# Low parts of eleven weight units per layer formed by accumulating transfers, and memsets that wait for the entry normalisation

## The chip, the cores and the metric

One core of a Trainium2 chip runs the whole program. The core has five engines with their own in-order instruction streams: PE (TensorE, the matmuls), DVE (VectorE), ACT (ScalarE), POOL (GpSimd) and SP, which here only issues transfers. The metric is the device time of one execution in microseconds (us); lower is better. Engines meet only through semaphores: an instruction waits until a counter has reached a value.

## The reference

Four normalisations and two layers over 512 tokens (two sequences of 256) of width 1024, all in float32. Each layer, cut to what matters here:

```
proj = h @ w_in                      # q, k, v, z, x/B/C, dt
attn = window_attention(rope(q), rope(k), v, sink)
xbc  = silu(depthwise_conv5(xbc))    # 12 tiles of 128 channels
y    = ssd(forward) + ssd(backward) + D * xs      # state space, chunks of 128
ssd_out = rms_norm(y * silu(z)) 
h = layer_norm(alpha * h + concat(attn, ssd_out) @ w_out)
h = layer_norm(alpha * h + (silu(conv3(h @ w_gate)) * (h @ w_val)) @ w_down)
```

## The kernel before

**Weights in units.** All weight matrices are cut into units of 128 x 1024 floats (512 KB). A layer has 105 units, numbered from 0: dt, k, v and q (0 to 6), the twelve convolved tiles (7 to 18), z (19 to 26), the output projection (27 to 38), up (39 to 82) and down (83 to 104). A ring of five slots (`RING = 5`) holds units in three forms: `raw` as loaded, `whi` (its rounded high part) and `wlo` (what is left, `raw - whi`). Each product is three matmuls: high by high, high by low, low by high. SP loads unit m into its slot once PE has finished unit m - 5 (`unit_used`); ACT copies `raw` into `whi` (function `split`, L595); DVE subtracts to give `wlo` (function `split`, L1285); PE waits for the count `unit_split` and multiplies.

**Slots.** A list of steps, `SCHED`, is written by `mixer_schedule`; each engine walks the same list and takes the steps that concern it, in that order. One slot n of the list surrounds the matmuls of unit n (step "G"). "SH" is ACT's high copy of a later unit (n + 4), "SL" DVE's low part, "S" both. In slots 19 to 26 of a layer (the z units) the state space part runs beside the projection. For each of its eight pairs i (a group of heads and a token block):

- SB (PE, L1166) and SF (PE, L1177) write exponents into four PSUM banks,
- SC (DVE, L1559, two instructions) caps them into `e_fwd` and `e_bwd`; SE (ACT, L759 twice and L765) takes the exponentials `e_fwd`, `e_bwd`, `e_off`,
- SW (DVE, L1564 and L1568) adds the two and multiplies by `cb`; SO (DVE, L1574) multiplies `e_off`,
- SD (PE, L1193) uses the results; SY (DVE, L1583) adds them up; SG (DVE, L1593) gates with z.

SB of pair i + 1 waits for all three exponentials of pair i. SD waits for SW and SO of its pair. A convolved tile goes: PE's product, ACT's centre tap (L693), four tap instructions on DVE (L1448), tanh on ACT ("SILU", L728), a product on DVE ("SIL2", L1455), and then a transposition on PE ("T", L1132), whose result ACT copies out (L746). POOL multiplies the same tile by D ("XS", L564) and builds the tiles `heads` ("MV", L575), 128 x 1024 each, in slots 15 to 17.

**Entry.** DVE normalises four token blocks of `hb` (L1342, L1345; `ln_normed` counts them), PE transposes them (L1033, L972), and POOL forms low parts (L531) and then clears three tiles with memsets (L546 to L548).

## Time and profile before

| what | value |
|---|---|
| median of 3 runs | 1307.52 us (1306.7 to 1307.57) |
| the profiled execution | 1307.72 us, of which the span is 1305.9 |
| PE busy | 1291.5 us (99% of the span) |
| DVE, ACT, POOL busy | 823.5, 580.6, 96.6 us |
| transfers | 129.24 MB, mean 99 GB/s |
| TensorE's granted clock | full speed, mean 0.999 |

The span is the time between the first and the last instruction; the 1.8 us beside it are around the program. The busy time of PE has modelled ends, so a stall shows as idle time only where it is longer than the tail of the matmul before it; the waits that the profile names are read for that.

### The profile page before, as it was taken

To read this page: it belongs to the slowest core of one execution; us is meant where nothing else is said; L and a number is where in the kernel's file an instruction comes from. 1 tells how busy PE (TensorE), PEld (TensorE's weight loads), DVE (VectorE), ACT (ScalarE), POOL (GpSimd) and SP (SyncE) were. 2 spreads that over 40 slices of the span, in tenths; PEclk is the share of its full clock that TensorE was granted. 3 is DMA by queue.
4 is the path that set the end of the run, shared out by engine and by line. 5 is a ranking of instruction groups with operands and counts; after the bars stand their busy time and mean duration, and the time that the engine had idled before them with its cause. 6 is when DMAs were issued, how large, how long until landed. Compare 5 with 4: busy or idle time off the path is not lost.

```text
span 1305.9 us, 16383 instructions
## 1 busy us (share of the span) xinstructions
PE 1291.5 (99%) x6688; PEld 1066.9 (82%) x6688; DVE 823.5 (63%) x1109; ACT 580.6 (44%) x875; POOL 96.6 (7%) x87
## 2 busy tenths in 40 slices
PE   9999999999999999999999999999999999999997
PEld 8877777889888888888898777778888888888886
DVE  7888799966444444342378987999654444443425
ACT  5766655436333333311276665544453333332112
POOL 2013400001000000000020234000000000000000
PEclk9999999999999999999999999999999999999999
DMA  5422212523333333333133212143233333333332
GB/s 188 163 68 56 65 59 65 182 62 126 96 97 98 96 99 95 128 98 97 55 129 135 65 50 81 52 143 113 82 98 97 98 97 97 97 97 128 98 97 112
DMA packets 33787, 129.24 MB, mean 99 GB/s; under 512 B 3793, under 2 KB 4209, under 8 KB 32561
## 3 DMA queue, kind: packets, MB, share of 16 engines
q1 hardware_dynamic: 33552, 127.91, 30.8%
q8 instruction: 53, 0.87, 0.3%
q0 software_dynamic: 160, 0.29, 0.1%
q14 instruction: 22, 0.17, 0.0%
HBM read 121.89 MB, written 6.29 MB: 98 GB/s over the span
## 4 chain that ended last, share of the span: by engine, by line
PE 90%; DVE 7%; issue 1%; ACT 1%; DMA 0%; DVEq 0%
PE ps L843 17%; PE ps L845 16%; PE ps L844 16%; PE ps L980 9%; PE ps L982 9%; PE ps L981 9%; PE ps L869 4%; PE ps L1193 1%; PE ps L1207 1%; PE ps L1217 1%; PE ps L1227 1%; DVE e_fwd L1559 1%; PE ps L972 1%; DVE e_fwd L1564 1%; DVE e_off L1574 1%
## 5 line engine op out<-in xcount | busy, mean ns | idle before, releaser
L843 PE MATMUL ps<-hhi,whi 128*128 128x512 f32 x1040 | 409.5, 394 | 0.0
L845 PE MATMUL ps<-hhi,wlo 128*128 128x512 f32 x1040 | 405.0, 389 | 0.0
L844 PE MATMUL ps<-hlo,whi 128*128 128x512 f32 x1040 | 404.8, 389 | 0.0
L1285 DVE TENSOR_TENSOR wlo<-raw,whi 128x1024 fp32r<-128x1024 f32 x208 | 253.9, 1222 | 150.3 <-ACT whi L595 150.3
L595 ACT ACTIVATE whi<-raw 128x1024 fp32r<-128x1024 f32 x208 | 219.3, 1056 | 218.0 <-DMA raw<-in_units 218.0
L843 PEld LDWEIGHTS ps<-hhi,whi 128*128 128x128 f32 x1040 | 195.2, 188 | 44.2 <-issue 4.9
L845 PEld LDWEIGHTS ps<-hhi,wlo 128*128 128x128 f32 x1040 | 195.2, 188 | 41.4
L844 PEld LDWEIGHTS ps<-hlo,whi 128*128 128x128 f32 x1040 | 195.3, 188 | 39.4
L980 PE MATMUL ps<-whi,uhi 128*128 128x512 f32 x352 | 137.1, 390 | 0.0
L982 PE MATMUL ps<-wlo,uhi 128*128 128x512 f32 x352 | 137.0, 389 | 0.0
L981 PE MATMUL ps<-whi,ulo 128*128 128x512 f32 x352 | 136.9, 389 | 0.0
L1660 DVE SCALAR_TENSOR_TENSOR gcv<-ps,pf,gcv 128x510 f32<-128x510 f32 x44 | 32.9, 748 | 157.2 <-ACT gcv L813 157.2
L813 ACT ACTIVATE gcv<-ps,pf 128x512 f32<-128x512 f32 x44 | 34.3, 780 | 168.9 <-PE ps L845 162.1
L1670 DVE TENSOR_TENSOR guf<-gsg,ps 128x512 f32<-128x512 f32 x44 | 30.2, 687 | 79.0 <-PE ps L845 78.4
L981 PEld LDWEIGHTS ps<-whi,ulo 128*128 128x128 f32 x352 | 66.1, 188 | 13.8
L982 PEld LDWEIGHTS ps<-wlo,uhi 128*128 128x128 f32 x352 | 66.1, 188 | 13.8
L980 PEld LDWEIGHTS ps<-whi,uhi 128*128 128x128 f32 x352 | 66.1, 188 | 13.5
L1448 DVE SCALAR_TENSOR_TENSOR cv<-ps,pm,cv 128x508 f32<-128x508 f32 (+1 forms) x96 | 71.4, 744 | 7.3 <-ACT cv L693 3.0
L980 PE MATMUL ps<-whi,ahi 128*128 128x512 f32 x192 | 75.8, 395 | 0.2
L981 PE MATMUL ps<-whi,alo 128*128 128x512 f32 x192 | 74.8, 389 | 0.0
L982 PE MATMUL ps<-wlo,ahi 128*128 128x512 f32 x192 | 74.8, 389 | 0.0
L531 POOL TENSOR_TENSOR hlo<-hfm,hhi 128x512 fp32r<-128x512 f32 x16 | 21.9, 1378 | 638.1 <-ACT hhi L630 637.8
(182 smaller groups left out, 1488.2 us busy)
## 6 DMA issues: line engine op xcount, KB each, us to landing
raw<-in_units SPq DMA_DIRECT2D x208, 512.0 KB, 3.7
gb<-in_gb SPq DMA_DIRECT2D x5, 1024.0 KB, 5.8
h_kept<-hb SPq DMA_DIRECT2D x2, 2048.0 KB, 9.2
ha<-h_kept SPq DMA_DIRECT2D x2, 2048.0 KB, 8.0
hb<-in_x SPq DMA_DIRECT2D x4, 512.0 KB, 5.9
out_y<-hb SPq DMA_DIRECT2D x8, 256.0 KB, 2.0
cn<-in_cn SPq DMA_DIRECT2D x1, 663.5 KB, 10.4
raw<-in_units SPq DMA_DIRECT2D x2, 128.0 KB, 3.5
```

The lines of the kernel that those rows point to most:

```text
L595: A(whi[:, m % RING, :], raw[:, m % RING, :], ACT.Copy).then_inc(unit_hi, 1)
L813: A(gcv[:], ps[:, bank, :], ACT.Identity, scale=pf[:, k * 3 + w0 + 1:k * 3 + w0 + 2], bias=pf[:, k + v0:k + v0 + 1]).then_inc(glu_center, 1)
L843: mm(out, whi[:, slot, cols], xhi, start=start, stop=False)
L844: mm(out, whi[:, slot, cols], xlo, start=False, stop=False)
L845: return mm(out, wlo[:, slot, cols], xhi, start=False, stop=stop)
L869: last = mm(out, w, x, start=c == 0 and kind == "hi hi", stop=stop, skip_group_check=True)
L980: mm(ps[:, bank, :], xhi[:, rows], whi[:, slot, cols], start=start, stop=False)
L981: mm(ps[:, bank, :], xlo[:, rows], whi[:, slot, cols], start=False, stop=False)
L982: return mm(ps[:, bank, :], xhi[:, rows], wlo[:, slot, cols], start=False, stop=stop)
L1285: V.tensor_tensor(wlo[:, m % RING, :], raw[:, m % RING, :], f(whi[:, m % RING, :]), ALU.subtract).then_inc(unit_split, 1)
L1448: V.scalar_tensor_tensor(out=dst[:, :, lo:hi], in0=src[:, :, lo + s:hi + s], scalar=pmc("conv_w", 5 * j + tap, 5 * j + tap + 1), in1=dst[: ...
L1660: V.scalar_tensor_tensor(out=dst[:, :, 1:SEQ], in0=src[:, :, 0:SEQ - 1], scalar=pf[:, k * 3 + w0:k * 3 + w0 + 1], in1=dst[:, :, 1:SEQ], op ...
```

## The change

`BY_DMA = range(20, 31)` names eleven units of each layer: z units 20 to 26 and the output projection's first four, 27 to 30. For these DVE does nothing. ACT, behind its copy into `whi`, waits for that copy and writes `-whi` into `wlo` (a second 128 x 1024 ACTIVATE). POOL waits for it (`low_minus`) and issues a transfer that adds the unit's floats from HBM onto `wlo` (`accum_op=ALU.add`); PE waits for that transfer's own semaphore, one for each ring slot. In the list of steps, DVE's remaining low parts (units 11 to 19) keep their places; in slots 19 to 25 "SO" now stands ahead of "SC", and in the last slot "SW" 7 stands at the slot's head as in the others. At the entry POOL waits for all four normalised blocks before its memsets. The waits of SB and SF are the same in both versions.

```diff
+BY_DMA = range(20, 31)
...
-        if U_Z <= n < U_OUT - 1:
+        if n >= U_Z:
             steps += [("SW", n - U_Z)]
...
-            if a == 0:
-                steps += [("SC", 1), ("SE", 4), ("SO", 0)]
-            elif a < 7:
-                steps += [("SO", a), ("SC", a + 1), ("SE", 3 * a + 4)]
-            else:
-                steps += [("SW", 7), ("SO", 7)]
-            steps += [("SL", n - 1 + AHEAD)]
+            steps += [("SO", a)]
+            if a < 7:
+                steps += [("SC", a + 1), ("SE", 3 * a + 4)]
...
+        def by_dma(m):
+            return m < DEPTH * UNITS and m % UNITS in BY_DMA
...
+        def wait_split(eng, m):
+            if by_dma(m):
+                eng.wait_ge(low_added[m % RING], 16 * sum(by_dma(n) and n % RING == m % RING for n in range(m + 1)))
+            else:
+                eng.wait_ge(unit_split, splits(m + 1))
...
                 if L == 0:
                     lows(0)
+                    pool.wait_ge(ln_normed, NBLK)
                 nc.gpsimd.memset(ln_dt[:, :, :, 1, :], 0.0).then_inc(ln_zeroed, 1)
...
-                    if what == "AN":
+                    if what in ("S", "SH") and by_dma(unit(L, i)):
+                        m = unit(L, i)
+                        pool.wait_ge(low_minus, adds(m + 1))
+                        pool.dma_start(wlo[:, m % RING, :], units[m], accum_op=ALU.add).then_inc(low_added[m % RING], 16)
+                    elif what == "AN":
...
                         A(whi[:, m % RING, :], raw[:, m % RING, :], ACT.Copy).then_inc(unit_hi, 1)
+                    if by_dma(m):
+                        act.wait_ge(unit_hi, m + 1)
+                        A(wlo[:, m % RING, :], f(whi[:, m % RING, :]), ACT.Copy, scale=-1.0).then_inc(low_minus, 1)
...
-                if m < DEPTH * UNITS:
+                if m < DEPTH * UNITS and not by_dma(m):
                     dve.wait_ge(unit_hi, m + 1)
```

ACT in slot 18, from the high copy of unit 22 on; before:

```order
L595 ACTIVATE whi<-raw 128x1024 [waits raw_loaded2]
L746 ACTIVATE xs_tm<-ps 128x4x128 [waits aux_full]
L759 ACTIVATE e_bwd<-e_bwd 128x1024 [waits capped]
L765 ACTIVATE e_off_95<-ps 128x1024 [waits seg_full]
L728 ACTIVATE xsc<-cv 128x512 [waits xd_done,aux_full,conv_taps]
L717 ACTIVATE zt<-ps 128x512 [waits unit_used]
```

And now:

```order
L618 ACTIVATE whi<-raw 128x1024 [waits raw_loaded2]
L621 ACTIVATE wlo<-whi 128x1024 [waits unit_hi]
L772 ACTIVATE xs_tm<-ps 128x4x128 [waits aux_full]
L785 ACTIVATE e_bwd<-e_bwd 128x1024 [waits capped]
L791 ACTIVATE e_off_95<-ps 128x1024 [waits seg_full]
L754 ACTIVATE xsc<-cv 128x512 [waits xd_done,aux_full,conv_taps]
L743 ACTIVATE zt<-ps 128x512 [waits unit_used]
```

One instruction has come in ahead of both exponentials and of the last tile's tanh.

DVE in slots 18 and 19, from the last SIL2 to the second pair's caps (SC 1: `e_fwd_93` and `e_bwd` from `ps`); before:

```order
L1455 SCALAR_TENSOR_TENSOR xsc<-xsc,cv 128x512 [waits conv_tanh]
L1285 TENSOR_TENSOR wlo<-raw,whi 128x1024 [waits unit_hi]
L1564 TENSOR_TENSOR e_fwd_92<-e_fwd_92,e_bwd 128x1024 [waits exp_done]
L1568 TENSOR_TENSOR e_fwd_92<-e_fwd_92,cb 128x1024 [waits w_sum,cb_done]
L1468 SCALAR_TENSOR_TENSOR zs<-zt,ps 128x512 [waits tanh_done,aux_full]
L1559 TENSOR_TENSOR e_fwd_93<-ps,cn 128x1024 [waits own_full]
L1559 TENSOR_TENSOR e_bwd<-ps,cn 128x1024
L1574 TENSOR_TENSOR e_off_95<-e_off_95,cb 128x1024 [waits exp_done]
L1285 TENSOR_TENSOR wlo<-raw,whi 128x1024 [waits unit_hi]
```

And now:

```order
L1481 SCALAR_TENSOR_TENSOR xsc<-xsc,cv 128x512 [waits conv_tanh]
L1590 TENSOR_TENSOR e_fwd_92<-e_fwd_92,e_bwd 128x1024 [waits exp_done]
L1594 TENSOR_TENSOR e_fwd_92<-e_fwd_92,cb 128x1024 [waits w_sum,cb_done]
L1494 SCALAR_TENSOR_TENSOR zs<-zt,ps 128x512 [waits tanh_done,aux_full]
L1600 TENSOR_TENSOR e_off_95<-e_off_95,cb 128x1024 [waits exp_done]
L1585 TENSOR_TENSOR e_fwd_93<-ps,cn 128x1024 [waits own_full]
L1585 TENSOR_TENSOR e_bwd<-ps,cn 128x1024
```

Two subtractions are gone, and the product of `e_off` has moved ahead of the two caps.

POOL in slots 15 to 18, where it builds `heads`; before:

```order
L575 TENSOR_TENSOR heads_81<-cum_a,cn 128x1024 [waits as_full,cum_done]
L564 TENSOR_TENSOR x_d_80<-xsc,pm 128x512 [waits silu_done]
L575 TENSOR_TENSOR heads_82<-cum_a,cn 128x1024
L575 TENSOR_TENSOR heads_83<-cum_a,cn 128x1024 [waits y_full]
L575 TENSOR_TENSOR heads_84<-cum_a,cn 128x1024 [waits aux_full]
L564 TENSOR_TENSOR x_d_80<-xsc,pm 128x512 [waits silu_done] x2
```

And now:

```order
L598 TENSOR_TENSOR heads_81<-cum_a,cn 128x1024 [waits as_full,cum_done]
L573 DMA wlo<-in_units 128x1024 [waits low_minus]
L587 TENSOR_TENSOR x_d_80<-xsc,pm 128x512 [waits silu_done]
L598 TENSOR_TENSOR heads_82<-cum_a,cn 128x1024
L573 DMA wlo<-in_units 128x1024 [waits low_minus]
L598 TENSOR_TENSOR heads_83<-cum_a,cn 128x1024 [waits y_full]
L598 TENSOR_TENSOR heads_84<-cum_a,cn 128x1024 [waits aux_full]
L587 TENSOR_TENSOR x_d_80<-xsc,pm 128x512 [waits silu_done]
L573 DMA wlo<-in_units 128x1024 [waits low_minus]
```

The last two `heads` now stand behind the transfer of unit 21, which waits for ACT.

## Rows read from the trace of the kernel before

**Rows 1.** The page, part 1: busy us (share of the span) and instructions of PE.

```profile
PE 1291.5 (99%) x6688; PEld 1066.9 (82%) x6688; DVE 823.5 (63%) x1109; ACT 580.6 (44%) x875; POOL 96.6 (7%) x87
```

**Rows 2.** Busy time by window: us, PE, PEld, DVE, ACT, POOL busy, clock, DMA share, GB/s.

```profile
150.00:230.00 80.00, 77.61 (x539) 61.57 (x539) 77.21 (x81) 42.00 (x50) 5.25 (x4) 1.00 0.21 62
```

**Rows 3.** Waits of PE: for whom, us in total, times, longest us.

```profile
PE ps L1193 <- DVE e_off L1574: 4.3, 4, 1.4
```

**Rows 4.** Timeline of PE around slot 19, first layer: start, us, [idle before].

```profile
161.35 0.66 PE L1132 MATMUL ps<-cn,xsc 128*128 128x128 f32 x4 [0.18 <-DVE xsc L1455]
...
167.96 0.61 PE L1177 MATMUL ps<-heads,off_w 128*128 128x512 f32 x2
170.00 0.44 PE L1193 MATMUL ps<-e_fwd,xs_tm 128*64 128x128 f32 x4 [1.43 <-DVE e_off L1574]
...
171.90 0.51 PE L1166 MATMUL ps<-heads,own_w 32*128 32x512 f32 x4
...
178.45 0.44 PE L1193 MATMUL ps<-e_fwd,xs_tm 128*64 128x128 f32 x4
```

**Rows 5.** Timeline of PE and DVE at the last pair's SD, first layer.

```profile
226.39 0.44 PE L1193 MATMUL ps<-e_fwd,xs_tm 128*64 128x128 f32 x4 [0.73 <-DVE e_off L1574]
...
224.92 1.22 DVE L1574 TENSOR_TENSOR e_off<-e_off,cb 128x1024 f32<-128x1024 f32 x1
```

**Rows 6.** Timeline of DVE at the entry, and PE behind it.

```profile
15.08 0.96 DVE L1345 TENSOR_SCALAR hb<-hb,st 128x1024 f32<-128x1024 f32 x1
...
16.15 2.76 DVE L1345 TENSOR_SCALAR hb<-hb,st 128x1024 f32<-128x1024 f32 x1
...
18.96 1.09 PE L972 MATMUL ps<-cn,hb 128*128 128x128 f32 x8 [0.82 <-DVE hb L1345]
```

**Rows 7.** Timeline of POOL at the entry.

```profile
6.17 0.70 POOL L542 DMA_DIRECT2D pm<-in_pm  x1 [5.23 <-DMA hb<-in_x]
...
14.18 2.99 POOL L531 TENSOR_TENSOR hlo<-hfm,hhi 128x512 fp32r<-128x512 f32 x2
...
17.41 0.95 POOL L548 MEMSET off_w<- 128x1024 f32 x1
```

**Rows 8.** Timeline of ACT, slots 17 to 19.

```profile
148.38 1.05 ACT L595 ACTIVATE whi<-raw 128x1024 fp32r<-128x1024 f32 x1
...
158.91 1.02 ACT L765 ACTIVATE e_off<-ps 128x1024 f32<-128x1024 f32 x1
159.94 0.63 ACT L728 ACTIVATE xsc<-cv 128x512 f32<-128x512 f32 x1
...
167.51 1.06 ACT L759 ACTIVATE e_fwd<-e_fwd 128x1024 f32<-128x1024 f32 x1 [4.27 <-DVE e_fwd L1559]
...
170.08 1.02 ACT L765 ACTIVATE e_off<-ps 128x1024 f32<-128x1024 f32 x1
```

**Rows 9.** Timeline of DVE, slots 17 to 19.

```profile
153.05 0.69 DVE L1455 SCALAR_TENSOR_TENSOR xsc<-xsc,cv 128x512 f32<-128x512 f32 x1 [0.70 <-ACT xsc L728]
...
161.22 1.22 DVE L1285 TENSOR_TENSOR wlo<-raw,whi 128x1024 fp32r<-128x1024 f32 x1
162.35 2.06 DVE L1564 TENSOR_TENSOR e_fwd<-e_fwd,e_bwd 128x1024 f32<-128x1024 f32 x1
...
168.52 1.22 DVE L1574 TENSOR_TENSOR e_off<-e_off,cb 128x1024 f32<-128x1024 f32 x1
```

**Rows 10.** Timeline of POOL, slots 17 and 18.

```profile
146.64 5.62 POOL L575 TENSOR_TENSOR heads<-cum_a,cn 128x1024 fp32r<-128x1024 f32 x3
...
161.38 1.96 POOL L564 TENSOR_TENSOR x_d<-xsc,pm 128x512 f32<-128x512 f32 x1 [6.51 <-DVE xsc L1455]
```

**Rows 11.** Transfers: the queue's packets, MB and share; issues: KB each, us to landing.

```profile
q1 hardware_dynamic: 33552, 127.91, 30.8%
...
raw<-in_units SPq DMA_DIRECT2D x208, 512.0 KB, 3.7
...
pm<-in_pm POOLq DMA_DIRECT2D x2, 80.0 KB, 4.0
```

More of the change, by code:

```diff
@@ L104, in mixer_schedule @@
             steps += [("AV", (i - 3) // 2)]
-        if U_CONV < n < U_Z - 1:
+        if U_CONV < n <= U_Z:
             steps += [("SL", n - 1 + AHEAD)]
@@ L154, in mixer_schedule @@
                 steps += [("XS", n - U_CONV)]
-            if n == U_Z - 1:
-                steps += [("SL", n - 1 + AHEAD)]
         if 15 <= n < 17:
@@ L165, in mixer_schedule @@
                 steps += [("SB", a + 1), ("SE", 3 * a + 3)]
-            if a == 0:
-                steps += [("SC", 1), ("SE", 4), ("SO", 0)]
-            elif a < 7:
-                steps += [("SO", a), ("SC", a + 1), ("SE", 3 * a + 4)]
-            else:
-                steps += [("SW", 7), ("SO", 7)]
-            steps += [("SL", n - 1 + AHEAD)]
+            steps += [("SO", a)]
+            if a < 7:
+                steps += [("SC", a + 1), ("SE", 3 * a + 4)]
+            if n >= U_Z:
+                steps += [("SL", n + AHEAD)]
             if a >= 1:
@@ L181, in mixer_schedule @@
     steps += [("GA", (U_OUT, (2, 3))), ("GA", (U_OUT, (0, 1))), ("SD", 7), ("SY", 7), ("SG", 7), ("GA", (U_OUT, (4, 5)))]
-    steps += [("RP", 1), ("RP", 3)] + [("SQ", c) for c in range(4, CT)] + [("RP", 5), ("RP", 7), ("SL", U_OUT - 1 + AHEAD)]
+    steps += [("RP", 1), ("RP", 3)] + [("SQ", c) for c in range(4, CT)] + [("RP", 5), ("RP", 7)]
     steps += [("GA", (U_OUT + 1, range(6))), ("GA", (U_OUT + 2, range(6))), ("RS", 0)]
@@ L346, in trunk @@
         y_scaled, y_ready = sem("y_scaled"), sem("y_ready")
+        low_minus = sem("low_minus")
+        low_added = [sem(f"low_added{k}") for k in range(RING)]
         h_low, h_lows, entry_low = sem("h_low"), sem("h_lows"), sem("entry_low")
@@ L419, in unit, with splits, adds @@
             return L * UNITS + n
+        def by_dma(m):
+            return m < DEPTH * UNITS and m % UNITS in BY_DMA
+        def splits(m):
+            return sum(not by_dma(n) for n in range(m))
+        def adds(m):
+            return sum(by_dma(n) for n in range(m))
+        def wait_split(eng, m):
[3 more added lines that the diff above has]
+                eng.wait_ge(unit_split, splits(m + 1))
         def wait_high(eng, idx, s, j):
@@ L933, in first_units @@
                 split_units = range(idx % 2 == 0, 2)
-                pe.wait_ge(unit_split, used + 1)
+                wait_split(pe, used)
                 for j in range(2):
@@ L938, in first_units @@
                         part(idx, used, 0, 0, kind, (2 * j, 2 * j + 1))
-                pe.wait_ge(unit_split, used + 2)
+                wait_split(pe, used + 1)
                 for kind in ("hi hi", "hi lo"):
@@ L952, in first_units @@
                 transposes(idx, 3)
-                pe.wait_ge(unit_split, used + 3)
+                wait_split(pe, used + 2)
                 for kind in ("hi hi", "hi lo", "lo hi"):
@@ L1018, in final_units @@
                             if t == 0 and half == 0:
-                                pe.wait_ge(unit_split, used + j + 1)
+                                wait_split(pe, used + j)
                             last = three_rows(2 * t + half, slot, xhi, xlo, False, j == FINAL - 1)
@@ L1057, in _ @@
                             pe.wait_ge(zs_done, L * CT + i - 2 - U_Z + 1)
-                        pe.wait_ge(unit_split, L * UNITS + i + 1)
+                        wait_split(pe, unit(L, i))
                         by_columns(unit(L, i) % RING, unit_bank(i))
@@ L1061, in _ @@
                         k = i - U_OUT
-                        pe.wait_ge(unit_split, L * UNITS + i + 1)
+                        wait_split(pe, unit(L, i))
                         before = None
@@ L1073, in _ @@
                     elif what == "GT":
-                        pe.wait_ge(unit_split, unit(L, U_UP))
+                        wait_split(pe, unit(L, U_UP) - 1)
                         pe.wait_ge(sl_done, L * CT + CT)
@@ L1081, in _ @@
                         u, banks = i
-                        pe.wait_ge(unit_split, L * UNITS + u + 1)
+                        wait_split(pe, unit(L, u))
                         if u == U_OUT and 2 in banks:
@@ L1246, in _ @@
                         n = U_UP + 2 * k + half
-                        pe.wait_ge(unit_split, unit(L, n) + 1)
+                        wait_split(pe, unit(L, n))
                         by_columns(unit(L, n) % RING, PAIR_BANK[k % 4] + half)
@@ L1251, in _ @@
                 for k in range(FT - count):
-                    pe.wait_ge(unit_split, unit(L, U_DOWN + k) + 1)
+                    wait_split(pe, unit(L, U_DOWN + k))
                     pe.wait_ge(glu_ready, L * FT + k + 1)
@@ L1263, in _ @@
                 if L < DEPTH - 1:
-                    pe.wait_ge(unit_split, unit(L, UNITS))
+                    wait_split(pe, unit(L, UNITS) - 1)
                 pe.wait_ge(glu_ready, L * FT + FT)
```

## The prediction, made before the changed kernel ran

> **What bounds the kernel now.** I read the page's busy times first. PE is busy for 1291.5 of 1305.9 us, DVE for 63% of the span [rows 1]. PE's busy time is a modelled one, so I go by its waits. The change can only win back what PE still waits; work taken from DVE is worth nothing by itself. TensorE's clock is granted in full in the window of [rows 2] (the 1.00 near the row's end), so no clock is to be had either.
>
> Second, the windows. In the 80 us of the state space slots PE is busy for 77.61 and DVE for 77.21 us [rows 2]. Here DVE is nearly full, and this is the stretch that the change aims at: 2.4 us of PE idle time per layer. At the entry there is one more wait.
>
> Third, who PE waits for. DVE's `e_off` (SO) holds SD up four times, 4.3 us in all [rows 3]. The timeline places them: 1.43 us ahead of the first pair's SD [rows 4], 0.73 us ahead of the last pair's SD [rows 5], and the same two in layer two, 2 x (1.43 + 0.73) = 4.3. The entry adds 0.82 us, where PE waits for the fourth normalised block [rows 6]. Then the transposition of the last convolved tile waits for 0.18 us [rows 4]. So the ceiling of the whole change is 4.3 + 0.8 + 0.4 = 5.5 us, 0.4% of the time. Within 0.2% (2.6 us) I call no change, which is about what a measurement of this kernel can tell.
>
> **The memsets at the entry.** The fourth block's normalisation takes 2.76 us, the third's 0.96, same shapes [rows 6]. While it stands, POOL ends its last subtraction (14.18 + 2.99 = 17.17) and goes straight on to the memsets, the largest until 17.41 + 0.95 = 18.36 [rows 7]; DVE ends at 18.91. With the memsets behind it, DVE has POOL in its way until 17.17 only and ends at about 17.17 + 0.9 = 18.1. PE could have taken the block at 18.96 - 0.82 = 18.14. So all of the 0.82 us goes: I take 0.8 and keep 0 as the other end, should POOL's subtraction and not the memsets be what held DVE. The memsets are wanted only some slots later; behind them on POOL stands nothing but the work of slot 8.
>
> **DVE's work taken away.** 11 subtractions a layer at 1.22 us [rows 9] are 13.4 us, about nine of them (11 us) in the window of [rows 2]. From then on DVE has 66 of 80 us to do. In its backlog lay the wait at the last pair: SO 7 ended at 224.92 + 1.22 = 226.14 [rows 5]. Eight subtractions before it are gone; even with new waits of a few us it is done before PE asks at 226.39 - 0.73 = 225.66. I take the whole 0.73 us per layer; it is the surest term in this stretch. The other end is 0.
>
> **ACT's added work.** 11 copies a layer into `wlo`. The shape's price is that of the copy into `whi`, 1.05 us [rows 8], and each waits for the copy ahead of it, so some 1.0 to 1.1 us is added to ACT each slot. ACT is busy for 42 of 80 us [rows 2], so in slots 20 to 26 this lies in idle time: it stands behind the third exponential, and the next cap is 4.27 us away [rows 8]. It is not covered in slot 18. There the new copy of unit 22 comes ahead of two exponentials and the last tile's tanh, which run back to back: `e_off` 158.91, `xsc` 159.94 [rows 8]. The tanh moves to about 160.95, SIL2 on DVE follows 1.0 us later, and PE's transposition, which waited for 0.18 us already, moves from 161.35 to about 162.35.
>
> From there two paths lead to slot 20. PE's own: SF was at 167.96 and comes at 168.96, SD about 0.5 us behind it (SF's 0.61 less the overlap) at 169.5, and SB of the next pair 1.90 us later (171.90 - 170.00, [rows 4]), at 171.4. SD no longer waits, since SO 0 now stands ahead of the caps. DVE's: SIL2 is 1.0 us later, but the subtraction behind it (161.22, 1.22 us, [rows 9]) is gone, so SW begins where it did, within 0.1 us. The product of `e_off`, about 1.1 us in a row of such instructions, now stands before the caps and not behind them, so the caps and the exponentials behind them come 1.0 to 1.1 us later: the third one, 170.08 before [rows 8], ends at about 171.1 + 1.02 = 172.1. SB of the next pair waits for it. It starts at about 172.2 to 172.3 against 171.90: 0.35 us later than before.
>
> So where the stall of 1.43 us goes, two come: about 1.0 us ahead of the transposition and 0.8 us ahead of SB. Slots 18 to 20 together cost +0.35 us per layer. The ends are -1.4 (no new wait counts) and +1.1 (the copy is not absorbed at all).
>
> **The transfers.** Each add waits on POOL for ACT's copy. Issuing costs POOL about 0.7 us [rows 7]. The margin is wide: unit 21's copy runs at 148.38 [rows 8], its `wlo` can be added to from about 150.5, and PE multiplies it only behind the SB of 171.90 [rows 4], 21 us later; the ring gives the others as much. A plain copy of 512 KB lands 3.7 us after its issue, and costs 30.8% x 1305.9 x 0.524 / 127.91 = 1.65 us of all sixteen engines [rows 11]. In a slot of 8.45 us (from SD at 170.00 to SD at 178.45, [rows 4]) an add may cost four times that beside the plain copy. No add is in this trace. The bounds are nothing, and POOL's own pace in the only transfers it has: 80 KB in 4.0 us [rows 11], so 25.6 us for 512 KB. I take it as hidden: most of those 4.0 us is latency, as the 3.7 us for 512 KB shows.
>
> **POOL's delayed work.** The transfer of unit 21 waits for ACT: 148.38 + 1.05 [rows 8], another 1.05 and some handing over, 150.55. With the issue it ends near 151.2, and the last two `heads` run from there, 5.62 / 3 = 1.87 us each [rows 10], to 153.1 and 155.0, not until 152.26 as before. They are needed slots later. But SIL2 of the tile before last starts at 153.05 [rows 9], and two such instructions disturb each other: POOL's product at 161.38 took 1.96 us beside DVE's subtraction [rows 9, 10], and DVE's sum right behind that took 2.06 us, where this shape otherwise takes 1.22. One waited for the other and then held it up. I take 0.2 us per layer, SIL2 waiting out the rest of the first of the two; the ends are 0 and 1.9 us. The Trainium skill says in SBUF — State Buffer, "Who interferes with whom", that a DVE instruction with two SBUF inputs and a GpSimd instruction that reads SBUF exclude each other for a whole instruction, while one that only writes does not disturb it. The durations just given agree with the first half. By the second half the moved memsets do not disturb the subtraction that they will stand beside; no run here shows that yet.
>
> **The sum.** Entry -0.8; per layer -0.73 + 0.35 + 0.2 = -0.18, so -0.4 for two. Together -1.2 us on the profiled 1307.72 us (span 1305.9 and 1.8 around it), which is 0.2 above the median. From the median: 1307.5 - 1.2 = 1306.3 us.
>
> **Rivals.**
>
> *All waits go.* ACT's copy could be absorbed in slot 18, and the exponentials be early enough. Then -0.8 - 4.3 = -5.1: 1302.4. For it: PE has no other waits listed in the stretch, and DVE becomes free. Against it: the tanh and the transposition were already back to back, with 0.18 us of waiting, and SB had only 171.90 - (170.08 + 1.02) = 0.8 us over the third exponential [rows 4, 8].
>
> *SIL2 waits for both `heads`.* If the second of them begins before 153.05, SIL2 stands until 155.0, 1.9 us late. SC 0, the first exponential, the centre tap of the last tile and with them SF 0 and all of slot 18 hang behind it on DVE and ACT, so PE loses nearly all of it: 2 x (1.9 - 0.2) = +3.4 on my sum, 1309.7. For it: at the entry DVE was not let in between POOL's subtraction and its memsets; the margin is 0.1 us. Against it: a slower issue of the transfer moves the second of the two behind SIL2's start. The skill's rule above is what makes this rival; by its "whichever starts first" the case turns on who asked earlier.
>
> *Slower, by the rate of the adds.* If an add holds the transfers for X us, the eleventh lands 11 X after the first's start, and PE wants it 21 + 10 x 8.45 = 105.5 us after: this decides from X = 9.6 us on. At X = 11.1, three times the plain landing, it costs 11 x 11.1 - 105.5 = 16.6 us per layer, 33 in all: 1339. At the bound of 25.6 it would be hundreds of us. For it: an accumulating transfer must read its target too. Against it: only 21% of the engines' time is used in the stretch [rows 2], and twice the plain 3.7 us, read and written again, is still under the mark.
>
> *Nothing of the stretch is won and the entry stays:* 1307.5; it lies inside my own range.
>
> **How the numbers follow.** The forecast with its neighbourhood (1305 to 1308) 0.45; all waits gone 0.20; both `heads` 0.25; adds too slow 0.07; nothing 0.03. The range that leaves about 0.2 out runs from 1303.2 to 1310.0: it takes in most of the second and third case and not the adds. Faster by over 0.2% (below 1304.9): nearly all of the second case and a little of the first, 0.24. Slower (above 1310.1): the adds, a third of the third case and a little beside, 0.17. The same: 0.59.
>
> **What the changed profile would show.** The fourth normalisation at about 1.8 us and no wait of 0.8 us on L972 at the entry: the memset step is right. No wait of SD on `e_off` in either place: DVE's relief is right. PE idle for about 1 us ahead of the last tile's transposition, and again ahead of SB at about 172: ACT's copy and the moved SO are priced right; if neither stands there, the second case holds. DVE's SIL2 at about 153 with over 2 us instead of 0.69: the third case. PE waiting on a transfer anywhere: the fourth. I would be wrong in kind if ACT waited for `raw` in slots 20 to 26, since there I left no cost at all.

## The result, and the profile after

The changed kernel takes 1309.73 us (median of 15 runs, 1309.35 to 1309.81), the kernel before 1306.93 us beside it (15 runs, 1306.63 to 1307.67). The ratio is 1.0019, with a 95% interval from 1.0012 to 1.0027: 2.5 us by the ratio. The times of the kernel before lie in two groups, near 1306.7 and near 1307.6, so its median differs by up to 1 us from one set of runs to the next; a difference of that size between kernels of two sets is read from traces below. The forecast was 1306.3 us, a gain of 1.2.

The first lines of the page, to be read against [rows 1]. DVE is 19 us less busy (22 subtractions fewer, and one product, named below, 4.7 us longer over the two layers), ACT 24 us more. PE is busy for 2.7 us longer with the same 6688 matmuls:

```profile
span 1307.9 us, 16405 instructions
PE 1294.2 (99%) x6688; PEld 1069.1 (82%) x6688; DVE 804.5 (62%) x1087; ACT 604.2 (46%) x897; POOL 114.1 (9%) x109
```

What PE waits for after the change (us in total, times, longest):

```profile
PE ps L1158 <- DVE xsc L1481: 3.2, 2, 1.6
PE ps L1203 <- DVE e_fwd L1585: 1.1, 2, 0.6
PE ps L883 <- POOL avg L552: 1.0, 1, 1.0
PE ps L1059 <- DVE hb L1371: 0.6, 1, 0.6
PE ps L1192 <- issue: 0.6, 2, 0.3
PE ps L998 <- DVE hb L1383: 0.2, 1, 0.2
```

All four waits of SD for `e_off`, 4.3 us [rows 3], are gone, and so are the 0.82 us at the entry. In their place come 3.2 us ahead of the transposition of the tile before last (L1158) and 1.1 us ahead of SF 0 (L1203). The timeline of POOL and then of DVE shows why (start, duration, what it is, and the idle time ahead):

```profile
149.62 0.90 POOL L573 DMA_DIRECT2D wlo<-in_units  x1 [2.99 <-ACT wlo L621]
150.22 4.08 POOL L598 TENSOR_TENSOR heads<-cum_a,cn 128x1024 fp32r<-128x1024 f32 x2
154.94 1.04 POOL L587 TENSOR_TENSOR x_d<-xsc,pm 128x512 f32<-128x512 f32 x1 [0.64 <-DVE xsc L1481]
```

```profile
151.84 3.02 DVE L1481 SCALAR_TENSOR_TENSOR xsc<-xsc,cv 128x512 f32<-128x512 f32 x1 [0.70 <-ACT xsc L754]
154.79 1.21 DVE L1585 TENSOR_TENSOR e_fwd<-ps,cn 128x1024 f32<-128x1024 f32 x1
155.92 1.21 DVE L1585 TENSOR_TENSOR e_bwd<-ps,cn 128x1024 f32<-128x1024 f32 x1
```

POOL waits 2.99 us for ACT's copy, issues the transfer of unit 21, and only then makes the last two `heads`. SIL2 asks at 151.84, while the first of them still runs, and ends 0.6 us behind the end of the second: 3.02 us in place of 0.69 [rows 9]. The same stands in layer two (3.01 us at 797.10). PE's timeline in layer one:

```profile
154.92 0.66 PE L1158 MATMUL ps<-cn,xsc 128*128 128x128 f32 x4 [1.60 <-DVE xsc L1481]
156.14 0.93 PE L1203 MATMUL ps<-heads,off_w 128*128 128x512 f32 x2 [0.57 <-DVE e_fwd L1585]
156.87 0.63 PE L869 MATMUL ps<-hhi,whi 128*128 128x512 f32 x1
157.29 0.63 PE L870 MATMUL ps<-hlo,whi 128*128 128x512 f32 x1
157.72 0.63 PE L871 MATMUL ps<-hhi,wlo 128*128 128x512 f32 x1
```

The last three rows are ordinary matmuls. They stand 0.43 us apart and last 0.63; ahead of the stall (152.02 to 152.93) they stand 0.23 apart and last 0.39. The windows give the reason in the number behind POOL's busy time, the granted clock: 0.57 over 4 us. It was at the lower of its two levels (1.2 of 2.4 GHz) for most of them. Here are the changed kernel's windows, then those of the kernel before, where it is 1.00:

```profile
150.00:156.00 6.00, 3.97 (x19) 2.85 (x17) 5.27 (x5) 0.63 (x1) 5.34 (x4) 1.00 0.77 160
156.00:160.00 4.00, 3.86 (x10) 3.06 (x11) 3.13 (x4) 3.94 (x5) 0.00 (x0) 0.57 0.05 22
```

```profile
150.00:156.00 6.00, 5.95 (x28) 4.75 (x28) 5.16 (x6) 1.72 (x3) 3.30 (x3) 1.00 0.12 12
156.00:160.00 4.00, 4.00 (x19) 3.31 (x18) 3.00 (x5) 3.99 (x6) 0.00 (x0) 1.00 0.30 113
```

PE counts as busy for 3.86 of 4 us and yet does 10 matmuls where it did 19. A loss of clock hides in the busy time; it is where most of PE's extra 2.7 us are from.

Both kernels issue the same 6688 matmuls in the same order, so their starts can be subtracted one by one. The steps of that difference (after less before, us), in the two layers; SB 2 is the SB of the third pair, which waits for the second pair's exponentials:

| place | layer one | layer two |
|---|---|---|
| entry, fourth block | -1.0 | |
| transposition of tile 10 | +1.7 | +1.7 |
| SF 0 | +0.6 | +0.6 |
| the half clock, 8 gaps of 0.43 | +1.6 | +1.6 |
| transposition of the last tile | -0.3 | -0.2 |
| SD 0 | -1.6 | -1.6 |
| SB 2 | +0.4 | +0.3 |
| SD 7 | -0.8 | -0.8 |

That is +1.6 per layer and -1.0 at the entry, with -0.2 from a load at the start: +1.9 between the two profiled executions.

**Did the half clock cost time?** The line of 1.6 in the table looks like it, but the changed kernel's 15 executions say no. Each has its mean granted clock on record:

| executions | mean clock | what it means | time, us |
|---|---|---|---|
| 5 | 0.996 | fell in both layers, as in the profile | 1309.57 to 1309.76 |
| 10 | 0.999 | as in the kernel before, where it did not fall | 1309.35 to 1309.81 |

Two falls of 3.4 us at the half level are 2 x 3.4 x 0.5 / 1308 = 0.0026 of the span, which is the difference between the two groups. The medians of their times are 1309.74 and 1309.73. Where the clock fell, PE was slow in a stretch behind which it would have waited, as e1 and g1 below show. So the fall is no part of the 2.5 us.

At the entry the fourth block's normalisation now takes 1.57 us against 2.76 [rows 6]:

```profile
14.90 0.96 DVE L1371 TENSOR_SCALAR hb<-hb,st 128x1024 f32<-128x1024 f32 x1
15.78 0.15 DVE L1377 RECIPROCAL st<-st 128x1 f32<-128x1 f32 x1
15.97 1.57 DVE L1371 TENSOR_SCALAR hb<-hb,st 128x1024 f32<-128x1024 f32 x1
17.47 1.21 DVE L1311 TENSOR_TENSOR wlo<-raw,whi 128x1024 fp32r<-128x1024 f32 x1
```

### The profile page after: what moved, and what is told of

It reads as the page before. It is cut to its first block, busy times and chain, and to the rows that moved or that the text cites. A ratio compares the mean times of both kernels' runs of the same rounds, so it can differ in the third digit from the quotient of the medians.

```text
span 1307.9 us, 16405 instructions
## 1 busy us (share of the span) xinstructions
PE 1294.2 (99%) x6688; PEld 1069.1 (82%) x6688; DVE 804.5 (62%) x1087; ACT 604.2 (46%) x897; POOL 114.1 (9%) x109
## 3 DMA queue, kind: packets, MB, share of 16 engines
q1 hardware_dynamic: 33552, 127.91, 30.0%
q0 software_dynamic: 3328, 11.82, 5.6%
## 4 chain that ended last, share of the span: by engine, by line
PE 96%; DVE 2%; ACT 1%; DMA 0%; POOL 0%; issue 0%; SPq 0%; DVEq 0%
PE ps L869 18%; PE ps L871 18%; PE ps L870 18%; PE ps L1006 9%; PE ps L1008 9%; PE ps L1007 9%; PE ps L895 5%; PE ps L1219 2%; PE ps L1233 1%; PE ps L1243 1%; PE ps L1253 1%; PE ps L998 1%; PE ps L1203 1%; PE ps L1166 1%; DMA raw<-in_units 0%; PE ps L1192 0%
## 5 line engine op out<-in xcount | busy, mean ns | idle before, releaser
L1311 DVE TENSOR_TENSOR wlo<-raw,whi 128x1024 fp32r<-128x1024 f32 x186 | 227.3, 1224 | 149.5 <-ACT whi L618 149.5
```

The costliest lines, as they stand in the source:

```text
L1311: V.tensor_tensor(wlo[:, m % RING, :], raw[:, m % RING, :], f(whi[:, m % RING, :]), ALU.subtract).then_inc(unit_split, 1)
```

## The experiments

Each kernel was timed in five rounds beside the kernel before. The theory: the delayed `heads` lock SIL2 out, and PE's idle time takes the clock. That its second half costs no time was shown above, and g1 shows it again. The main rival: the loss is carried by ACT's copies and the transfers themselves, and the lock is only where it shows.

**The `heads` ahead of the transfer (e1).** In the changed kernel:

```
-            steps += [("AV", 3)]
+            steps += [("AV", 3), ("MV", 2), ("MV", 3)]
...
-            if n == 17:
-                steps += [("MV", 2), ("MV", 3)]
```

> The changed kernel, with POOL's last two `heads` of the `x`/`dt` products moved ahead of the transfer of unit 21, so that they no longer wait for ACT's negated copy and run where they ran before the change. My theory (the subtraction-like SIL2 of the tile before last was locked out through both `heads`, 3.02 us instead of 0.69, and the idle time this gave PE let the clock fall): SIL2 takes about 0.7 us again, PE's wait of 1.6 us ahead of the transposition of tile 10 goes, the granted clock stays at 1.00 in slot 17 and 18, and the time falls to 1304.5 to 1306.5 us. The rival (ACT's eleven added copies and the transfers themselves carry the loss, the lock is only where it shows): the time stays within 1 us of 1309.7.

1305.05 us, ratio 0.9982 (0.9973 to 0.9992). The same transfers and copies, one place exchanged on POOL, and 4.7 us less than the changed kernel. POOL, then DVE:

```profile
146.81 3.75 POOL L596 TENSOR_TENSOR heads<-cum_a,cn 128x1024 fp32r<-128x1024 f32 x2
150.51 0.87 POOL L571 DMA_DIRECT2D wlo<-in_units  x1
```

```profile
152.05 0.69 DVE L1479 SCALAR_TENSOR_TENSOR xsc<-xsc,cv 128x512 f32<-128x512 f32 x1 [0.70 <-ACT xsc L752]
```

SIL2 takes 0.69 us, the clock is 1.00 in both windows. The main rival has fallen. Against the kernel before, layer one now steps +0.9 (last tile), -1.5 (SD 0), +0.6 (SB 2), -0.8 (SD 7). The changed kernel's trace less this one gives the price of the lock: 1.7 + 0.6 us of new waits per layer, 1.6 of half clock, and almost as much of waits that then fall away. The net is 2.3.

**The memsets alone (e2).** In the kernel before, `pool.wait_ge(ln_normed, NBLK)` ahead of the memsets.

> The kernel before, with only the wait of POOL's entry memsets for the fourth normalised block. My theory: the fourth block's subtraction on DVE takes 1.6 to 1.8 us and not 2.76, PE's 0.82 us ahead of it go, and nothing else moves: 0.8 to 1.0 us faster than before, about 1306.0. The rival (POOL's subtraction and not the memsets held DVE): no change, 1306.9.

1306.55 us, ratio 0.9995 (0.9986 to 1.0004). The interval includes no change, so the time alone doesn't show the 0.8 to 1.0 expected. The trace does: PE starts on the fourth block about 1 us earlier, and stays 1.16 us ahead to the end (part of that from an earlier load); the normalisation takes 1.57 us.

**The lock alone (e3).** In the kernel before, with no transfer at all:

```
                         elif i == 2:
                             wait_y_full(pool, L, ("AP", 6, 1))
+                            pool.wait_ge(conv_taps, L * 4 * N_CONV + 4 * 10 + 2)
```

> The kernel before, with no added transfers and DVE's subtractions all in place; only POOL's last two `heads` wait until DVE has issued the second tap of tile 10, so that they begin shortly before SIL2 of the tile before last (about 151 us in layer one). If the lock alone does it: SIL2 stands for both `heads`, 2 to 3 us in place of 0.69, PE waits 1.2 to 1.8 us ahead of the transposition of tile 10, and if PE's idle time is what takes the clock, the clock falls to half for some us behind it: 1.2 to 3 us per layer, 1309.3 to 1313. If the transfers or ACT's copies are needed for the loss: 1306.9, unchanged.

1309.54 us, ratio 1.0020 (1.0011 to 1.0028). POOL, DVE, and the window of the clock:

```profile
149.77 3.76 POOL L576 TENSOR_TENSOR heads<-cum_a,cn 128x1024 fp32r<-128x1024 f32 x2 [2.33 <-DVE cv L1449]
```

```profile
151.96 2.11 DVE L1456 SCALAR_TENSOR_TENSOR xsc<-xsc,cv 128x512 f32<-128x512 f32 x1 [0.70 <-ACT xsc L729]
```

```profile
156.00:160.00 4.00, 4.00 (x19) 3.27 (x18) 3.09 (x5) 4.00 (x6) 0.00 (x0) 1.00 0.08 33
```

The lock does it without any transfer: SIL2 asks just behind the start of the second product and takes 2.11 us, PE steps back by 0.8 + 0.6 = 1.4 us per layer, and nothing behind gives it back. The clock stays. With 0.7 and 0.57 us of PE idle time it doesn't fall; in the changed kernel's profile, with 1.6 and 0.57, it did. The time lies in the range expected, but what it was to be made of did not come: a wait of 1.2 to 1.8 us and a fall of the clock.

**ACT's copy of unit 22 behind the last tanh (e4).** On top of e1:

```
-                    if by_dma(m):
+                    if by_dma(m) and m % UNITS != 22:
...
                         A(dst, cv[:, i % 2, :], ACT.Tanh, scale=0.5).then_inc(conv_tanh, 1)
+                        if i == 11:
+                            minus(unit(L, 22))
```

> As the first of these runs (the last two `heads` ahead of the transfer of unit 21), and in addition ACT's negated copy of unit 22 is moved behind the tanh of the last tile, so that it no longer stands ahead of that tanh. My theory: the wait ahead of the transposition of the last tile (0.7 us) and a part of SB's wait in slot 19 go as well, and all of DVE's old waits stay away: 1301 to 1303.5 us, 4 to 6 us faster than before. The rival (PE's waits there are set by DVE or by the caps, not by ACT's copy): the same as the first run, within 0.7 us.

1303.94 us, 0.9975 (0.9965 to 0.9985), just above the range expected. The last tile's transposition comes 0.97 us earlier than in e1, once per layer; that much the copy cost. But SB 2 gives 0.44 of it back, and its wait grows:

```profile
PE ps L1196 <- issue: 1.9, 2, 1.0
```

**The caps of the second pair ahead of SO 0 (f1).** On top of e4: `("SC", 1), ("SE", 4), ("SO", 0)` for `a == 0`.

> As the run with the late copy of unit 22, and in addition the caps of the second pair stand ahead of `e_off`'s product (SC 1, SE 4, SO 0) in slot 19, as they did before the change. There SB of the next pair waits 1.0 us per layer, because the third exponential ends at 170.1 us, behind caps that begin at 165.3 though PE had filled their bank earlier. My theory: the caps come 1.1 us earlier, that wait goes, and SD of the first pair waits at most 0.4 us: 0.6 to 1.0 us less per layer, 1302.0 to 1302.8. The rival (it only trades one wait for the old one ahead of SD): within 0.4 us of 1303.9.

1303.04 us, 0.9970 (0.9959 to 0.9981). Half a miss: SB 2 comes 1.04 us earlier, as expected, but SD 0 comes 0.59 later. The net of 0.45 per layer lies below the 0.6 to 1.0 expected. It is read from the traces; the intervals of e4 and f1 overlap. The change's new place of SO 0 was bought with SB's wait, more than one for one (1.04 for 0.59). SO 0 is the only one that the change moved ahead of its caps: in slots 20 to 25 SO stood there before.

**The change without its transfers (f3).** The changed kernel with `BY_DMA = range(20, 20)`: DVE makes all low parts.

> The changed kernel with its new order of steps and the memset wait, but without any transfer: DVE makes all low parts, ACT makes no negated copies, POOL waits for nothing new. It tells what DVE's relief is worth. The kernel of the first batch that has the relief and not the delayed `heads` runs in 1305.05 us, the kernel with the memset wait alone in 1306.55. My theory: the wait of the last pair's SD on `e_off` (0.8 us) is still there, the wait of the first pair's SD is gone or short because SO 0 stands earlier, and SB waits for its caps instead, 1 to 2 us: no gain on the memsets alone, 1306.0 to 1308.0. The rival (the order of the steps brings the gain, and the transfers are worth nothing): 1305.0 or less.

1307.70 us, 1.0004 (0.9996 to 1.0013). The new order alone wins nothing: the medians put it 1.15 us behind e2, which has the same memset wait. The two intervals overlap, but the traces differ by the same 1.15. The transfers, in this order and where they don't delay the `heads` (e1), are worth 1307.70 - 1305.05 = 2.65 us (intervals apart); against the old order (e2) they and the new one together are worth 1.5 (1.4 by the traces). One part of the expectation failed: SD 7's wait of 0.8 us is gone here too, though DVE makes all low parts. The order alone takes it away, since SW 7 now stands at the slot's head; in its place PE loses 0.6 us per layer just ahead, on a matmul of the output projection:

```profile
224.28 0.47 PE L1006 MATMUL ps<-whi,ahi 128*128 128x512 f32 x1 [0.45 <-issue]
```

**When is DVE let in between two products?** e3 left a gap: there SIL2 met only the second product, in the changed kernel the first, and still it had to let both pass. I first moved the two later in the kernel before, with a memset and a wait for it (f2; the wait is e3's):

```
+                            nc.gpsimd.memset(f(heads[2][:, 0:3, :]), 0.0).then_inc(pad, 1)
+                            pool.wait_ge(pad, L + 1)
```

> As the run with the lock alone (the kernel before, no transfers, POOL's last two `heads` held back), but held back half a microsecond longer by a small memset, so that SIL2 of the tile before last meets the first of the two and not the second. In that run SIL2 took 2.11 us, PE waited 0.7 and 0.57 us, and the granted clock stayed at 1.00. If SIL2 is locked out through both products, it takes 2.6 to 3.1 us here; if PE's idle time is what lets the clock fall, PE then waits 1.2 to 1.7 and 0.6 us and the clock falls to half for some us behind it: 1311 to 1314. If the clock's fall came from the transfers or anything else in the changed kernel, the clock stays at 1.00 and the time is 1310.0 to 1311.5. If DVE is let in between the two products, as the order of asking would have it: SIL2 takes about 2.2 us and the time stays near 1309.5.

1307.12 us, 1.0004 (0.9996 to 1.0013): the third expectation had the right kind and the wrong size: SIL2 took not even 2.2 us, and the time is 2.4 below the 1309.5 given. It ran between the two, and the second product waited for it (4.21 us for two against 3.76). POOL, then DVE:

```profile
150.81 0.42 POOL L575 MEMSET heads<- 128x384 f32 x1 [2.30 <-DVE cv L1452]
151.31 4.21 POOL L579 TENSOR_TENSOR heads<-cum_a,cn 128x1024 fp32r<-128x1024 f32 x2
```

```profile
153.02 0.74 DVE L1459 SCALAR_TENSOR_TENSOR xsc<-xsc,cv 128x512 f32<-128x512 f32 x1 [0.70 <-ACT xsc L732]
```

Next a small plain transfer in the memset's place (g1), `pool.dma_start(pad_t[:], pm_d[L][:, 0:8])`, into a tile that nothing reads, without a wait for it:

> As the run in which a memset stood ahead of the two held back `heads`, but with a small plain transfer (8 columns into a tile that nothing reads) in the memset's place. There DVE's SIL2, which asked 0.15 us before the second `heads`, was let in between the two and took 0.74 us; in the changed kernel it was not, and there the instruction ahead of the two was a transfer, with the first of the two starting 0.3 us before the transfer's own record ends and each of them lasting 2.2 and not 1.9 us. Theory one (behind a transfer POOL hands its next instructions over earlier, so that the second is there before the first ends): SIL2 takes 3 us here, PE waits 1.6 to 1.7 and 0.57 us ahead of the transposition of tile 10 and of SF 0, +2.3 us per layer, 1311.0 to 1312.0 if the clock stays at 1.00, and 1313.5 to 1315 if that idle time alone lets the clock fall as in the changed kernel. Theory two (the size of the accumulating transfer, or something else in the changed kernel, did it): SIL2 takes 0.7 to 0.8 us and the time is 1306.5 to 1307.5.

1312.50 us, 1.0038 (1.0025 to 1.0051), between the two ranges of theory one and in neither. POOL, DVE, the clock:

```profile
150.78 0.58 POOL L576 DMA_DIRECT2D pad_t<-in_pm  x1 [2.75 <-DVE cv L1452]
151.38 3.76 POOL L579 TENSOR_TENSOR heads<-cum_a,cn 128x1024 fp32r<-128x1024 f32 x2
```

```profile
152.54 3.16 DVE L1459 SCALAR_TENSOR_TENSOR xsc<-xsc,cv 128x512 f32<-128x512 f32 x1 [0.70 <-ACT xsc L732]
```

```profile
156.00:160.00 4.00, 3.43 (x12) 2.54 (x11) 3.23 (x4) 3.13 (x5) 0.82 (x1) 0.64 0.21 85
```

So the kernel before shows the whole of the loss, with a transfer of 8 columns: SIL2 locked out through both, PE idle for 1.69 and 0.57 us, and the clock down in layer one. In layer two PE lost nearly the same (steps of 1.87 and 0.58 against 1.88 and 0.57), and the clock did not fall. This prices the fall within one execution. Ahead of SD 0 PE waits 0.21 us in layer one, behind the half clock, and 1.43 in layer two:

```profile
171.95 0.44 PE L1197 MATMUL ps<-e_fwd,xs_tm 128*64 128x128 f32 x4 [0.21 <-DVE e_off L1578]
818.47 0.44 PE L1197 MATMUL ps<-e_fwd,xs_tm 128*64 128x128 f32 x4 [1.43 <-DVE e_off L1578]
```

Layer one steps by 1.6 for the clock and then by -0.3 (last tile) and -1.2 (SD 0), layer two by none of them. From tile 10 to behind SD 0 either layer loses 2.4 us against the kernel before. The half clock used up waits that PE had anyway. The reason I gave for the lock, that POOL holds the second product ready early, has no support here: the two stand back to back (3.76 us), not overlapped by 0.3 us as in the changed kernel.

Then f2's memset and wait in the changed kernel, between the transfer of unit 21 and the two `heads` (g3):

> The changed kernel, with a small memset (and a wait for it) between the transfer of unit 21 and the two `heads`, as in the run where DVE was let in. The `heads` begin 0.4 us later than in the changed kernel, so that by time alone SIL2 should fare worse. Theory one (the transfer right ahead makes the two `heads` inseparable): the first of them starts at about 150.6 and lasts 1.9 us, SIL2 is let in at about 152.5 and takes 1.3 to 1.5 us, PE waits about 0.3 us ahead of the transposition of tile 10, the clock stays at 1.00, and the time is 1305.0 to 1306.5. Theory two (SIL2 is locked out whenever it asks this early): SIL2 takes 3.4 us, and the time is 1310 to 1312.

1306.94 us, 0.9997 (0.9988 to 1.0006). SIL2 takes 1.63 us and is let in, though it asks 1.1 us before the first product ends; the time lies 0.4 above what I gave. The trace has a wait of 0.6 us ahead of SF 0 in each layer that I had left out.

Memset or wait? Four tiny memsets and no wait, in the kernel before (h2), and g1's transfer one tap earlier with a wait for the third tap behind it (h3):

> As the run with the memset ahead of the two held back `heads`, but the memset is four tiny ones into a tile that nothing reads, and no wait on them stands ahead of the first of the two. So far SIL2 of the tile before last was let in between the two `heads` in both runs that had a memset and a wait for it right ahead of them, and locked out through both in both runs (the changed kernel too) that had a transfer right ahead. If the transfer makes the difference: SIL2 is let in between the two here, takes 0.7 to 1.5 us, 1306.5 to 1308.5 us. If the wait in front of the first makes it: SIL2 is locked out through both, about 3 us, and the time is 1311 to 1313.

> As the run with the small plain transfer ahead of the two held back `heads`, but the transfer is issued one tap earlier, and between it and the first of the two POOL waits for DVE's third tap. SIL2 asks some 1.3 to 1.5 us after the first of the two has begun. If the transfer must stand right ahead, or a wait in front of the first of the two is what parts them: SIL2 is let in after the first, takes 1.0 to 1.4 us, 1306.5 to 1308.5 us. If any transfer shortly ahead makes POOL keep the two together: about 3 us, 1311 to 1313.

h2, 1310.25 us, 1.0023 (1.0013 to 1.0032), lies in neither range and tells nothing on this: SIL2 asked 0.18 us after the second product had begun and took 2.26 us, e3's case again. h3, 1308.56 us, 1.0007 (0.9998 to 1.0016): let in, 1.05 us. The time is 0.06 above what I gave.

The last two set h2's time right with eighteen memsets (h4), and put a wait alone into the changed kernel (h5):

```
                             wait_y_full(pool, L, ("AP", 6, 1))
+                            pool.wait_ge(conv_taps, L * 4 * N_CONV + 4 * 10 + 3)
```

> As the run with four tiny memsets and no wait ahead of the two held back `heads`, but with eighteen of them, so that the first product begins about 0.5 us later and SIL2 asks 0.3 to 0.5 us before it ends (in that run it asked 0.18 us after the second had begun, and told nothing). If a wait right ahead of the first product is what parts the two: SIL2 is locked out through both, 2.9 to 3.1 us here, PE waits 1.5 to 1.7 us, 1311 to 1313 us. If only a transfer right ahead keeps them together: SIL2 is let in after the first, 1.0 to 1.2 us, 1306.5 to 1308.5 us.

> The changed kernel, with nothing but a wait (for DVE's third tap of tile 10) between the transfer of unit 21 and the first of the two `heads`, which then begins 0.2 to 0.3 us later. If a transfer shortly ahead is enough to keep the two together: SIL2 takes 3.0 to 3.3 us, the clock falls again, 1309.5 to 1311 us. If the wait parts them, as in the three runs where DVE was let in: SIL2 is let in at about 152.4 and takes 1.1 to 1.4 us, PE's wait of 1.6 us ahead of the transposition of tile 10 goes, the clock stays at 1.00, and the time is 1305.3 to 1307.0 us.

h4: 1307.74 us, 1.0002 (0.9993 to 1.0011). No wait and no transfer, and DVE is let in (0.80 us, where I gave 1.0 to 1.2). h5: 1306.06 us, 0.9990 (0.9981 to 0.9999), 3.7 us less than the changed kernel and in the range expected. POOL and DVE in h5:

```profile
149.76 0.90 POOL L573 DMA_DIRECT2D wlo<-in_units  x1 [2.98 <-ACT wlo L622]
150.66 4.25 POOL L599 TENSOR_TENSOR heads<-cum_a,cn 128x1024 fp32r<-128x1024 f32 x2
```

```profile
151.99 1.17 DVE L1482 SCALAR_TENSOR_TENSOR xsc<-xsc,cv 128x512 f32<-128x512 f32 x1 [0.70 <-ACT xsc L755]
```

SIL2 asks while the first product runs, as in the changed kernel, and gets in between. All cases in which it asked within the first of the two, the same in both layers:

| kernel | ahead of the two products | SIL2, us | let in |
|---|---|---|---|
| changed | transfer | 3.02 | no |
| g1 | small transfer | 3.16 | no |
| f2 | memset, wait | 0.74 | yes |
| g3 | transfer, memset, wait | 1.63 | yes |
| h3 | small transfer, wait | 1.05 | yes |
| h4 | memsets | 0.80 | yes |
| h5 | transfer, wait | 1.17 | yes |

In the two kernels where the two `heads` came right behind a transfer, with no wait between, they were not parted; in the five others they were. It is not the moment of asking: g1's SIL2 asked 1.16 us after the first product's start, between g3's (0.81) and h3's (1.39), which were let in. It is not the distance from the transfer either: the first product begins at the end of the transfer's record in g1 (151.36 and 151.38) as in h5 (150.66). What is left is the wait or the memsets between. Why POOL behaves so is not shown.

Nor is a transfer needed everywhere. In the kernel before, DVE's fourth normalisation asked at 16.15, during POOL's last subtraction (until 17.17), and stood until behind the three memsets that followed at once (until 18.36), with no transfer near [rows 6, 7]. So the table speaks for these two products and no more.

**The best kernel (g5).** f1 in which POOL's `x_d` of the last tile waits for the first cap of the second pair:

```
+                        if i == 11:
+                            pool.wait_ge(capped, 2 * (L * 8 + 1) + 1)
```

> The best kernel so far (`heads` ahead of the transfer, late copy of unit 22, caps of the second pair ahead of SO 0), and in addition POOL's product `x_d` of the last tile waits for the first cap of the second pair. In the best kernel it starts at 161.21, between two DVE products with two SBUF inputs, the second of which then takes 2.32 us instead of 1.22; PE later waits 0.54 us for `e_off`. My theory: that product takes 1.22 us, all DVE work behind it in slot 19 is 1.1 us earlier, and the 0.54 us per layer go: 1301.8 to 1302.3. The rival (the caps wait for ACT or PE and not for DVE, or `x_d` now holds up SO 0): within 0.3 us of 1303.0.

1301.91 us, ratio 0.9958 (0.9944 to 0.9972): the fastest of all, 5.7 us under the kernel before beside it, and in the range expected. DVE's product that `x_d` used to hold up, in f1 and then in g5, and all that PE still waits for in g5:

```profile
161.34 2.32 DVE L1601 TENSOR_TENSOR e_fwd<-e_fwd,cb 128x1024 f32<-128x1024 f32 x1
```

```profile
161.03 1.23 DVE L1603 TENSOR_TENSOR e_fwd<-e_fwd,cb 128x1024 f32<-128x1024 f32 x1
```

```profile
PE ps L892 <- POOL avg L553: 1.0, 1, 1.0
PE ps L1167 <- DVE xsc L1490: 0.3, 2, 0.2
PE ps L1007 <- DVE hb L1392: 0.2, 1, 0.2
```

## Why the prediction was wrong

**The step that failed** is the term "POOL's delayed work", taken at 0.2 us per layer with 0 and 1.9 as its ends. It measured 2.35: (1309.73 - 1305.05) / 2, the changed kernel against e1; 2.3 by the traces. The mechanism was seen and stood among the rivals ("SIL2 waits for both `heads`", a chance of 0.25, 1309.7 us). What the forecast had wrong is the wait: "SIL2 waiting out the rest of the first of the two". I let it hang on a margin of 0.1 us, whether the second product began before SIL2 asked. It did not: its record begins at 152.09, 0.25 us after SIL2's, and by my reasoning SIL2 had to wait out the first one only. It waited out both. PE then lost 1.7 + 0.6 = 2.3 us per layer, where my bound was 1.9.

The rival's 1309.7 us came so near to the measured 1309.73 by luck. Its base, my sum without any lock, was 1306.3 - 0.4 = 1305.9, and e1 has 1305.05: 0.85 too high. Its lock was 2 x 1.9 = 3.8 us, and 4.7 were measured: 0.9 too low.

**TensorE's clock** was read as "granted in full" and put aside, and no rival had a term for it. In the profile it fell for 3.4 us in each layer. Leaving it out did the number no harm: 1.6 us per layer of slow matmuls stand against 1.5 to 1.6 of waits that fall away (the last tile's transposition steps by -0.3 where e1 has +0.9, SD 0 and SB 2 by 0.3 less than in e1), and the executions without the fall took as long.

**The memsets**: right in the traces, 0.8 us forecast and 1.0 there; by e2's time alone it is not shown. The normalisation ended 0.55 us behind POOL's subtraction (16.99 and 17.54), where I had taken 0.9.

**DVE's relief**: right in number, 0.8 us against 0.73, and only in part for the reason given. In f3 SD 7's wait goes without any relief, by the new place of SW 7, and 0.6 us come just ahead of it; the relief takes away those 0.6. **ACT's copy and SO 0's place**: right in kind. In e1, without the lock, the last tile's transposition is 0.9 us later (forecast 1.0), SD 0's wait is gone, and SB 2 steps by +0.6 (forecast 0.8); slots 18 to 20 sum to 0.0 where I had +0.35. With the lock gone the change is worth 1305.05 against 1307.54, more than the 1.2 us of my sum (1.6 without its term for the lock).

**The transfers**: right. Nothing in slots 20 to 26 waits for them. The page gives issue to landing:

```profile
raw<-in_units SPq DMA_DIRECT2D x208, 512.0 KB, 3.6
wlo<-in_units POOLq DMA_DIRECT2D x22, 512.0 KB, 5.6
```

5.6 us is far below the 9.6 from which they would have decided.

**The Trainium skill's rule** (SBUF — State Buffer, "Who interferes with whom"), by which the two sorts of instruction exclude each other and the first to ask goes first, agrees in part. In every case of the table, in e3 and in h2, SIL2 ended 0.54 to 0.57 us behind the end of one of POOL's products: it never ran beside one. "First to ask" does not cover the changed kernel and g1, where DVE asked during the first product, before the second one's record begins, and came behind both. Its other half, that a GpSimd instruction which only writes disturbs no such DVE instruction, agrees: POOL's memsets (17.60 to 18.85) now lie beside DVE's subtraction, which takes 1.21 us as elsewhere.

## What to carry to other kernels

A wait added to one engine's queue moves all that stands behind it. Look up what those instructions will now lie beside, on engines that exclude each other with theirs, and put what needs no wait ahead of the waiting one. Between a POOL transfer and POOL work beside which DVE must get its turn, put a wait or a memset, and see in the trace whether it parts them. Read the granted clock in windows, since a lower clock shows as busy time, not as waiting. But before you price it, ask whether PE would have waited behind that stretch anyway, and compare the executions in which it fell with those in which it did not: here the price was nothing.

## What the runs showed of the hardware

- A DVE product with two SBUF inputs stood for 3.02 and 3.16 us instead of 0.69 when it asked in the first of two POOL products that came right behind a transfer; with a wait or memsets there it took 0.74 to 1.63. In each case it ended 0.54 to 0.57 us behind the end of a POOL product.
- The granted clock fell to its half level for about 3.4 us (0.57 over 4 us: 4 x 0.43 / 0.5), right behind PE idle times of 1.6 and 0.57 us, in both layers of the changed kernel's profile and in one layer of g1's. It did not fall in g1's other layer with the same idle times, nor, by the mean clock of 0.999, in 10 of the changed kernel's 15 executions, nor in any profile with 0.8 and 0.57. Such an idle time is not enough by itself; what else it takes stays open. The changed kernel took the same time with the fall and without (1309.74 and 1309.73 us).
- An accumulating transfer of 512 KB landed 5.6 us after its issue (a plain one 3.6) and held POOL for 0.9 us. The queue of the 22 of them (11.82 MB with four small loads) took 5.6% of the span, where the queue of the plain ones took 30.0% for 127.91 MB: about twice as much per byte.

```profile
q1 hardware_dynamic: 33552, 127.91, 30.0%
q0 software_dynamic: 3328, 11.82, 5.6%
```
